# A two-network transformer stack in fp32 on one core: layer norm tile by tile, its affine part folded into the modulation columns

## The chip, the cores and the metric

The kernel is one program on one core of a Trainium2 chip. The metric is the device time of one execution in microseconds (us); the median over runs is compared. TensorE (PE) multiplies, VectorE (DVE) and ScalarE (ACT) do elementwise work, GpSimd (POOL) does a little of it and issues some transfers, SyncE (SP) only issues transfers.

## The reference

256 tokens of width 1024 pass through two networks, all in fp32.

```python
def _post_norm(x, y, gate, res_w, gain, bias):
    return _layer_norm(ALPHA * x + res_w * (1.0 + gate) * y, gain, bias)

for l in range(2):                                   # first network
    y = _swiglu(_modulate(x, sh1, sc1), ffn1...)     # 1024 -> 2816 -> 1024
    x = _post_norm(x, y, g1, 0.5, gain0, bias0)
    y = _token_mixer(_modulate(x, sh2, sc2), w_in, w_out)
    x = _post_norm(x, y, g2, 1.0, gain1, bias1)
    y = _swiglu(_modulate(x, sh3, sc3), ffn2...)
    x = _post_norm(x, y, g3, 0.5, gain2, bias2)
```

`_modulate(x, shift, scale)` is `x * (1 + scale) + shift`. Shift, scale and gate of each stage are rows of 1024 numbers: a condition vector times a 1024 x 1024 matrix, plus a bias. `_layer_norm` subtracts the mean of a token's 1024 numbers, multiplies with the inverse root of their variance, then multiplies with `gain` and adds `bias`. The second network has four more such stages: an attention and pooling mixer, a mixture of 16 experts that each take 32 of the 256 tokens (3 matrices of 1024 x 1024 per expert), a short convolution, and a second mixture of experts. Each ends in the same kind of post norm: ten in all.

## The kernel before

**Layout.** `x_tok` holds the residual, two token tiles (`t` = 0, 1) of 128 tokens by 1024. A stage needs it turned: PE transposes 128 x 128 blocks into PSUM banks 4 to 7, and ACT (banks 4, 5) and DVE (banks 6, 7) write them to `uT` with the modulation applied as a scale and a shift per partition (`turn`, L1020 on ACT, L1294 on DVE). For an FFN they write it twice, once in fp32 and once rounded to fp32r (`u_hi`), and DVE forms the difference `u_lo`; each product is then three fp32r products, high by high, low by high, high by low (L631, L643).

**Stages.** In order: FFN, mixer, FFN, FFN, mixer, FFN, attention mixer, experts, convolution, experts. The stage's result is summed in PSUM banks 0 to 3 (two per token tile). In the FFN loop, 22 hidden tiles run as gate/up (48 matmuls, L631) and down (12 matmuls, L643); ACT rounds the weights (`high_gate_up`, L1047), DVE takes the remainder (`low_gate_up`, L1347), and DVE also computes the modulation rows of later stages between them (L1263). `times_rows` (L668) is the output projection of a mixer: the chunk of the inner dimension is its outer loop, both token tiles are its inner one.

**Norm.** `norm(p, acc, ...)` on DVE waits for the whole sum, and then does each step for both token tiles before the next step: gate product (L1311), residual (L1315), statistics (L1319, L1322), variance plus epsilon (L1324), centre and gain (L1326), root on ACT (L1028), reciprocal (L1328), inverse root and bias (L1335). Then PE turns `x_tok` (L612), and ACT and DVE evacuate. ACT loads the bias row into `gate_row` when the gate product is done (L1026). `columns` (L1277) adds one to the scale.

**Queues.** SP issues the weights in program order with waits for free slots: `step_weights` for an FFN step (slots 0 to 2 and 3 to 5 in turn), `mod_chunk` for quarters of a modulation matrix (`W_mod`, two buffers), slots 6 to 11 for a mixer's 16 loads. A `mod_chunk` with `c == 0` first waits for `mod_taken`, that is, for DVE's sum of the row before (L1273), since it also loads `mod_bias`. In a mixer these quarters are multiplied on PE (`mod_quarter`, L589) between the projections (L688). POOL issues the shift and scale columns (L517), the gate and gain rows (L526, L527), and copies the condition for the next modulation job (`set_cond`, L532). The high and low weight parts (`parts`) lie over slots 8 to 11, `tmp` and `scr`. The two layers of the first network are a hardware loop on every engine.

## Time and profile before

| | |
|---|---|
| runs | 2713.0, 2719.28, 2723.32 us; median 2719.28 |
| profiled execution | 2719.25 us, its span 2717.6 |
| PE, DVE, ACT, POOL busy | 78%, 37%, 19%, 2% of the span |
| transfers | 758 MB, 279 GB/s over the span |

Busy time is a mean over stages with different limits; the windows below are cut at the stages' ends. PEclk is the TensorE clock that was granted, as a share of 2.4 GHz: 0.50 is its lower level, 1.2 GHz. In a timeline row the bracket gives the idle time before the instruction and what ended it; a row with a count merges instructions that follow each other.

### The profile page before, as it was taken

How to read it: one execution, taken by the hardware profiler on the slowest of the kernel's cores; microseconds unless marked ns; L12 is line 12 of the kernel's file. 1: busy time of each engine (PE TensorE's matmuls, PEld its weight loads, DVE VectorE, ACT ScalarE, POOL GpSimd, SP SyncE). 2: the span in 40 equal slices, each digit the busy share in tenths (PEclk: the TensorE clock that was granted, in tenths of full speed). 3: DMA queues.
4: the chain of work that ended last, by engine and by line, in shares of the span. 5: the costliest groups of instructions: out<-in, count | busy, mean ns of one | idle time of the engine just before them, and what ended most of it. 6: DMA issues, size and time to landing. Idle time of an engine off the chain costs nothing.

```text
span 2717.6 us, 34800 instructions
## 1 busy us (share of the span) xinstructions
PE 2130.7 (78%) x12924; PEld 1346.4 (50%) x12924; DVE 1009.7 (37%) x1599; ACT 506.8 (19%) x782; POOL 52.7 (2%) x83
## 2 busy tenths in 40 slices
PE   2899786799799798779977687777777967666665
PEld 1889345499699734469965332222225732111111
DVE  0777214578787702377734310000003131000002
ACT  0433012233333202133313110000000010000000
POOL 1000000000000000000010000000000000000000
PEclk8999897899899998889998787777778979888887
DMA  6787647178768663648862289999998339999997
GB/s 215 260 293 255 244 167 263 57 280 294 266 232 309 246 220 145 217 147 309 306 205 78 93 308 410 410 409 410 410 410 269 140 141 410 410 410 410 410 410 281
DMA packets 288864, 758.06 MB, mean 279 GB/s; under 512 B 17104, under 2 KB 124912, under 8 KB 288672
## 3 DMA queue, kind: packets, MB, share of 16 engines
q1 hardware_dynamic: 282368, 737.34, 72.0%
q0 software_dynamic: 5168, 16.05, 1.8%
q10 hardware_dynamic: 1264, 3.80, 0.4%
q8 instruction: 42, 0.69, 0.1%
q14 instruction: 22, 0.18, 0.0%
HBM read 755.94 MB, written 1.18 MB: 279 GB/s over the span
## 4 chain that ended last, share of the span: by engine, by line
PE 44%; DMA 24%; SPq 13%; DVE 9%; issue 4%; DVEq 4%; ACT 1%; ACTq 0%; POOL 0%; POOLq 0%
DMA W<-in_w_exp_up 16%; PE psum L631 13%; SPq L461 11%; PE psum L688 6%; PE psum L643 6%; DMA W_mod<-in_mod_w 5%; PE psum L668 4%; PE psum L987 3%; PE psum L589 2%; PE psum L926 2%; DVE parts L1347 2%; DMA W<-in_w_exp_down 1%; PE psum L828 1%; DVE mod_acc L1263 1%; SPq L465 1%
## 5 line engine op out<-in xcount | busy, mean ns | idle before, releaser
L631 PE MATMUL psum<-parts 128*128 128x256 f32 x4224 | 528.3, 285 | 43.3 <-DVE parts L1294 41.1
L631 PEld LDWEIGHTS psum<-parts 128*128 128x128 f32 x4224 | 524.0, 194 | 53.5 <-issue 42.1
L926 PE MATMUL psum<-W,scr 128*32 128x512 f32 x2048 | 305.8, 704 | 155.5 <-DMA W<-in_w_exp_up 151.3
L643 PE MATMUL psum<-parts 128*128 128x512 f32 x1056 | 257.7, 393 | 0.0
L926 PEld LDWEIGHTS psum<-W,scr 128*32 128x32 f32 x2048 | 52.3, 116 | 380.0 <-DMA W<-in_w_exp_up 304.2
L1347 DVE TENSOR_TENSOR parts<-W,parts 128x1024 fp32r<-128x1024 f32 x176 | 207.4, 1222 | 77.6 <-ACT parts L1047 77.6
L1682 DVE TENSOR_TENSOR scr<-scr,psum 128x256 f32<-128x256 f32 x32 | 13.5, 421 | 584.4 <-ACT scr L1212 584.4
L951 PE MATMUL psum<-W,scr 128*32 128x256 f32 x2048 | 177.1, 495 | 67.9 <-DMA W<-in_w_exp_down 52.7
L643 PEld LDWEIGHTS psum<-parts 128*128 128x128 f32 x1056 | 192.6, 188 | 45.2 <-issue 6.6
L1263 DVE SCALAR_TENSOR_TENSOR mod_acc<-W_mod,cond,mod_acc 128x1024 f32<-128x1024 f32 x140 | 179.9, 1285 | 56.9 <-DMA W_mod<-in_mod_w 36.7
L1047 ACT ACTIVATE parts<-W 128x1024 fp32r<-128x1024 f32 x176 | 175.8, 1051 | 107.5 <-issue 65.0
L688 PE MATMUL psum<-W,uT 128*128 128x512 f32 x384 | 177.5, 615 | 2.7 <-DVE uT L1294 2.7
L963 PE MATMUL psum<-scr 128*128 128x512 f32 x256 | 145.1, 719 | 31.7 <-DVE scr L1694 29.7
L951 PEld LDWEIGHTS psum<-W,scr 128*32 128x32 f32 x2048 | 71.8, 139 | 164.3 <-DMA W<-in_w_exp_down 86.4
L1212 ACT ACTIVATE scr<-psum 128x256 f32<-128x256 f32 x32 | 12.3, 383 | 599.4 <-PE psum L926 599.4
L1694 DVE COPY scr<-psum 32x256 f32<-32x256 f32 x64 | 27.3, 426 | 258.3 <-PE psum L951 257.9
L688 PEld LDWEIGHTS psum<-W,uT 128*128 128x128 f32 x384 | 73.2, 197 | 97.6 <-issue 95.1
L612 PE MATMUL psum<-k_ident,x_tok 128*128 128x128 f32 x160 | 36.2, 405 | 102.9 <-DVE x_tok L1335 101.6
L963 PEld LDWEIGHTS psum<-scr 128*128 128x128 f32 x256 | 57.0, 235 | 114.3 <-issue 61.7
L1356 DVE TENSOR_TENSOR parts<-W,parts 128x1024 fp32r<-128x1024 f32 x88 | 107.2, 1219 | 8.5 <-ACT parts L1056 8.5
L589 PE MATMUL psum<-W_mod,cond_now 128*32 128x256 f32 x768 | 61.6, 453 | 52.5 <-DMA W_mod<-in_mod_w 35.4
L1056 ACT ACTIVATE parts<-W 128x1024 fp32r<-128x1024 f32 x88 | 92.8, 1055 | 47.7 <-DVE mod_out L1273 18.5
(263 smaller groups left out, 1706.1 us busy)
## 6 DMA issues: line engine op xcount, KB each, us to landing
W_mod<-in_mod_w SPq DMA_DIRECT2D x128, 1024.0 KB, 6.5
W<-in_w_exp_down SPq DMA_DIRECT2D x128, 1024.0 KB
W<-in_w_exp_gate SPq DMA_DIRECT2D x256, 512.0 KB, 14.2
W<-in_w_exp_up SPq DMA_DIRECT2D x256, 512.0 KB, 15.7
W<-in_ffn_w_gate SPq DMA_DIRECT2D x44, 1024.0 KB, 9.5
W<-in_ffn_w_up SPq DMA_DIRECT2D x44, 1024.0 KB, 12.3
W<-in_ffn_w_down SPq DMA_DIRECT2D x44, 1024.0 KB, 10.1
W<-in_w_in SPq DMA_DIRECT2D x24, 1024.0 KB, 7.5
```

The source lines that it names most:

```text
L461: sp.dma_start(W[:, s, D * n:D * n + D], w[layer, ds(e, 1), P * s:P * s + P, :] .rearrange("a p n -> p (a n)")).then_inc(landed[s], 16)
L589: ins = pe.matmul(psum[32 * q:32 * q + 32, bank, 0:256], cond_now[:, 2 * c + kk, :], part(W_mod[:, c % 2, :], 0, 2, D)[:, kk, 256 * q:256 ...
L631: ins = pe.matmul(psum[:, 4 + t % 2, S * g:S * g + S], w[:, t % 2, g, kc, :], u[:, kc, :], start=(n == 0 and kc == 0), stop=(n == 2 and kc ...
L643: ins = pe.matmul(psum[:, 2 * tt + h, :], h_[:, t % 2, P * tt:P * tt + P], w[:, t % 2, 512 * h:512 * h + 512], start=(t == 0 and n == 0), ...
L668: ins = pe.matmul(psum[:, 2 * tt + h, :], src[:, kc, P * tt:P * tt + P], w[:, kk, 512 * h:512 * h + 512], start=(kc == 0), stop=(kc == KC ...
L688: ins = pe.matmul(psum[:, 4 + n % 4, :], uT[:, kc, P * t:P * t + P], part(W[:, s, :], 0, 4, 512)[:, kc % 4, :], start=(kc == 0), stop=(kc ...
L926: ins = pe.matmul(psum[32 * q:32 * q + 32, 4, :].rearrange("p (g n) -> p g n", g=2), xe_now[:, kc, :], w[:, :, q, :], start=(kc == 0), sto ...
L951: ins = pe.matmul(psum[32 * q:32 * q + 32, 6, 0:256], e_hT[:, c % 2, 32 * (c // 2):32 * (c // 2) + 32], part(W[:, s, :], 0, 2, D)[:, c % 2 ...
L963: ins = pe.matmul(psum[:, 2 * tt + h, :], GT[:, P * tt:P * tt + P], R[:, 512 * h:512 * h + 512], start=first, stop=True, skip_group_check= ...
L1047: ins = act.activation(gu_hi[:, t % 2, g, :, :], part(W[:, b + g, :], 0, KC, STEP)[:, :, P * (t % 2):P * (t % 2) + P], copy)
L1263: ins = dve.scalar_tensor_tensor(mod_acc[:, :], w, col, mod_acc[:, :], mul, add)
L1347: ins = dve.tensor_tensor(gu_lo[:, t % 2, g, :, :], part(W[:, b + g, :], 0, KC, STEP)[:, :, P * (t % 2):P * (t % 2) + P], gu_hi[:, t % 2, ...
```

## The change

- **Norm by token tile.** `norm` does gate product and moments of tile 0, then the gate product of tile 1, writes tile 0 of `x_tok`, then the moments of tile 1, and writes tile 1. The sum of tile 0 has a semaphore of its own (`acc_t0`), and `times_rows` finishes tile 0 before it begins tile 1.
- **No gain and no bias in it.** `x_tok` is written as (tmp - mean) * inverse root, by one `tensor_scalar`. `columns` builds `u_scale` = (1 + scale) * gain and `u_shift` = (1 + scale) * bias + shift from columns of 8 numbers per partition, and the evacuations use these. Only the last norm applies gain and bias itself.
- **`finish_x` on GpSimd** multiplies `x_tok` with the gain row and adds the bias row (four 128 x 1024 `tensor_tensor`, with a transfer of the bias row between them) once the stage has read the normalized `x_tok`; the next norm waits for it (`x_biased`).
- **Turning by tile.** PE turns tile 0 as soon as it is written; ACT alone evacuates its eight blocks (`turn_first`), and ACT and DVE share those of tile 1 (`turn_tiles`), which in an FFN are followed by one rounding of half of `uT` each.
- **Early weight parts.** A mixer's `w_out` goes to slots 0, 1, 2, 6, so that ACT and DVE form the high and low parts of the next FFN's first two tiles before the norm; in the same way between the two FFNs that follow each other (`then`). The second step of the FFN behind a mixer is loaded once the mixer's sum is done.
- **`mod_bias`** and the wait for `mod_taken` go from the first quarter of a modulation job to its last.
- The loop over the two layers is written out; PE turns the first tile of x between the context's products of the attention mixer.

The diff, cut to its core:

```diff
-MIX_S = (6, 7, 8, 9, 10, 11)
-MIX_SLOTS = len(MIX_S)
 MIX_IN_USES = IN_W * D // (P * 2048)
 MIX_USES = MIX_IN_USES + D * D // (P * 2048)
-PER_LAYER = [sum(1 for u in range(MIX_USES) if u % MIX_SLOTS == s) for s in range(MIX_SLOTS)]
+MIX_S = tuple(6 + u % 6 for u in range(MIX_IN_USES)) + (0, 1, 2, 6)
 SLOTS = 12
+UT_TURNS = [0, 1, 3, 4, 5, 7, 9, 10, 11, 12]
...
-                if c == 0:
+                if c == 3:
...
-                step_weights(l, k, 0, 0, base)
+                step_weights(l, k, 0, 0, max(base - 2, 1))
+                if k == 1:
+                    sp.wait_ge(m_pe.s, m_pe.at("out", l))
...
+            def finish_x(s, *read):
+                for r in read:
+                    pool.wait_ge(*r)
+                pool.wait_ge(gain_landed, s * 16)
+                for t in range(TT):
+                    ins = pool.tensor_tensor(x_tok[:, t, :], x_tok[:, t, :], gain_row[:, :], ALU.mult)
+                ins.then_inc(x_gained, 1)
+                pool.wait_ge(x_gained, s)
+                row(s, "ln_b", lnb_landed)
+                pool.wait_ge(lnb_landed, s * 16)
+                for t in range(TT):
+                    ins = pool.tensor_tensor(x_tok[:, t, :], x_tok[:, t, :], gain_row[:, :], ALU.add)
+                ins.then_inc(x_biased, 1)
...
+            columns(0, 0, 16 * 2)
+            for l in range(LAYERS):
+                mix_job = l * JOBS_LAYER + (FIRST_JOBS + PAIRS)
                 for k in range(3):
-                    turned = l * 4 + (1 + (k if k < 2 else 3))
-                    pool.wait_ge(tr_act, turned)
-                    pool.wait_ge(tr_dve, turned)
-                    columns(l * 9 + 3 * k, l * (9 * 16) + 16 * (3 * k + 2))
-                    rows(l * 3 + k, l * 9 + (3 * k + 2), l * (9 * 16) + 16 * (3 * k + 3))
+                    s = 3 * l + k
+                    if s:
+                        finish_x(s, (tr_pe, 16 * l + 4 * (0, 1, 3)[k] + 4))
+                        pool.wait_ge(x_biased, s)
+                    if s < 5:
+                        row(s + 1, "ln_g", gain_landed)
+                    gate(s, 9 * l + 3 * k + 2, 16 * (9 * l + 3 * k + 3))
+                    if k == 1:
+                        for j in range(1, PAIRS):
+                            set_cond(mix_job + j)
+                    if s < 5:
+                        columns(s + 1, 9 * l + 3 * k + 3, 16 * (9 * l + 3 * k + 5))
                     if k == 0:
-                        set_cond(l * JOBS_LAYER + (FIRST_JOBS + PAIRS))
-                    if k == 1:
-                        with pool.Fori(1, PAIRS) as j:
-                            set_cond(l * JOBS_LAYER + j + (FIRST_JOBS + PAIRS))
+                        set_cond(mix_job)
...
+            for s in range(6, 10):
+                at = MOD2 + 3 * (s - 6)
+                finish_x(s, *(((r_pe.s, r_pe.at("s7", (s - 7) // 2)),) if s in (7, 9) else ((tr_pe, 4 * (s + 3) + 4),)))
+                pool.wait_ge(x_biased, s)
+                row(s + 1, "ln_g", gain_landed)
+                gate(s, at + 2)
+                if s < 9:
+                    columns(s + 1, at + 3)
...
+            def turn_tile(ready, t):
+                pe.wait_ge(pn_x, ready)
+                for kc in range(KC):
+                    c = P * (kc % 4)
+                    ins = pe.transpose(psum[:, 4 + 2 * t + kc // 4, c:c + P], x_tok[:, t, P * kc:P * kc + P], ident[:, :])
+                    if kc % 4 == 3:
+                        ins.then_inc(tr_pe, 1)
...
+                at = []
+                for tt in range(TT):
+                    for kc in range(KC):
+                        if tt == 0 and kc % 2 == 0:
+                            at.append(slots(kc // 2))
+                        w = part(W[:, at[kc // 2], :], 0, 2, D)
+                        for h in range(2):
+                            ins = pe.matmul(psum[:, 2 * tt + h, :], src[:, kc, P * tt:P * tt + P],
+                                            w[:, kc % 2, 512 * h:512 * h + 512], start=(kc == 0), stop=(kc == KC - 1),
+                                            skip_group_check=True)
+                    if tt == 0:
+                        ins.then_inc(acc_t0, 1)
...
+                turn_tile(13 + t, t)
                 s = in_slot("in", MIXIN_S[2]) if t == 0 else MIXIN_S[2]
+                if t == 0:
+                    pe.wait_ge(pn_var, 11)
...
+            def turn_tiles(inst, s, split=False):
+                act.wait_ge(tr_pe, inst * 4 + 3)
+                for kc in range(KC // 2):
+                    src = psum[:, 6, P * kc:P * kc + P]
+                    ins = act.activation(uT[:, kc, P:S], src, copy, bias=u_shift[:, kc:kc + 1], scale=u_scale[:, kc:kc + 1])
+                if split:
+                    act.drain()
+                    ins = act.activation(u_hi[:, 0:4, :], uT[:, 0:4, :], copy)
+                ins.then_inc(tr_act, 1)
+            def turn_first(inst, s):
+                act.wait_ge(cols_ready, s + 1)
+                for kc in range(KC):
+                    if kc % 4 == 0:
+                        act.wait_ge(tr_pe, inst * 4 + kc // 4 + 1)
+                    src = psum[:, 4 + kc // 4, P * (kc % 4):P * (kc % 4) + P]
+                    ins = act.activation(uT[:, kc, 0:P], src, copy, bias=u_shift[:, kc:kc + 1], scale=u_scale[:, kc:kc + 1])
+                ins.then_inc(tr_first, 1)
+            def root(s, t):
+                act.wait_ge(pn_var, 2 * s + t + 1)
+                act.activation(rstd[:, t:t + 1], inv[:, t:t + 1], ACT.Sqrt).then_inc(pn_sqrt, 1)
+            def norm_turn(s, inst, split=False):
+                root(s - 1, 0)
+                turn_first(inst, s)
+                root(s - 1, 1)
+                turn_tiles(inst, s, split)
...
+                if then is not None:
+                    high_gate_up(*then, 0)
                 silu(TILES - 1)
+                if then is not None:
+                    high_gate_up(*then, 1)
...
+            def columns(s, evacuated=None):
+                dve.wait_ge(cols_landed, s * 64 + 32)
+                if evacuated is not None:
+                    dve.wait_ge(*evacuated)
+                if s:
+                    dve.scalar_tensor_tensor(u_scale[:, :], scale_c[:, :], 1.0, gain_c[:, :], add, mul)
+                    dve.scalar_tensor_tensor(u_shift[:, :], scale_c[:, :], 1.0, bias_c[:, :], add, mul)
+                    dve.drain()
+                    dve.tensor_tensor(u_shift[:, :], u_shift[:, :], shift_c[:, :], add).then_inc(cols_ready, 1)
...
+            def turn_tiles(inst, split=False):
+                dve.wait_ge(tr_pe, inst * 4 + 4)
+                for kc in range(KC // 2, KC):
+                    src = psum[:, 7, P * (kc % 4):P * (kc % 4) + P]
+                    ins = dve.tensor_scalar(uT[:, kc, P:S], src, u_scale[:, kc:kc + 1], u_shift[:, kc:kc + 1], mul, add)
+                if split:
+                    dve.wait_ge(tr_first, 1 + UT_TURNS.index(inst))
+                    dve.drain()
+                    ins = dve.tensor_copy(u_hi[:, 4:8, :], uT[:, 4:8, :])
...
+            def norm(s, summed, alpha, res, eps, last=False):
+                dve.wait_ge(rows_landed, s * 16 + 16)
                 if res is not None:
                     dve.tensor_scalar(gate_row[:, :], gate_row[:, :], 1.0, res, add, mul)
                     dve.drain()
...
+                if last:
+                    dve.wait_ge(gain_landed, 160)
+                    dve.wait_ge(lnb_late, 16)
+                def gated(t):
+                    dve.wait_ge(*summed[t])
+                    dve.tensor_tensor(part(tmp[:, t, :], 0, 2, 512), psum[:, 2 * t:2 * t + 2, :], part(gate_row[:, :], 0, 2, 512), mul)
+                def moments(t):
+                    dve.drain()
                     dve.scalar_tensor_tensor(tmp[:, t, :], x_tok[:, t, :], alpha, tmp[:, t, :], mul, add)
...
+                    dve.drain()
                     for h in range(2):
                         dve.bn_stats(stats[:, 2 * t + h, :], tmp[:, t, 512 * h:512 * h + 512])
...
+                    dve.drain()
                     dve.bn_aggr(mv[:, t, :], stats[:, 2 * t:2 * t + 2, :])
...
+                    dve.drain()
+                    dve.tensor_scalar(inv[:, t:t + 1], mv[:, t, 1:2], eps, None, add).then_inc(pn_var, 1)
+                def scaled(t):
+                    dve.wait_ge(pn_sqrt, 2 * s + t + 1)
+                    dve.reciprocal(inv[:, t:t + 1], rstd[:, t:t + 1])
+                    if last:
+                        dve.scalar_tensor_tensor(tmp[:, t, :], tmp[:, t, :], mv[:, t, 0:1], gain_row[:, :], sub, mul)
+                        dve.drain()
+                        dve.scalar_tensor_tensor(x_tok[:, t, :], tmp[:, t, :], inv[:, t:t + 1], bias_late[:, :], mul, add
+                                                 ).then_inc(pn_x, 1)
+                    else:
+                        dve.drain()
+                        dve.tensor_scalar(x_tok[:, t, :], tmp[:, t, :], mv[:, t, 0:1], inv[:, t:t + 1], sub, mul).then_inc(pn_x, 1)
+                gated(0)
+                if s:
+                    dve.wait_ge(x_biased, s)
+                moments(0)
+                gated(1)
+                scaled(0)
+                moments(1)
+                scaled(1)
...
+            for l in range(LAYERS):
+                s = 3 * l
+                turn_tiles(4 * l, split=True)
                 ffn(l, 0)
-                norm(l * 3, (pe_down, l * (2 * TILES) + (1 + TILES)), ALPHA, 0.5, LN_EPS)
-                turn(l * 4 + 1, l * 3 + 1)
+                columns(s + 1, (tr_act, 4 * l + 2))
+                norm(s, ((acc_t0, s + 1), (pe_down, l * (2 * TILES) + (1 + TILES))), ALPHA, 0.5, LN_EPS)
+                turn_tiles(4 * l + 1)
                 mixer(l)
-                norm(l * 3 + 1, (m_pe.s, m_pe.at("out", l)), ALPHA, 1.0, LN_EPS)
-                ffn(l, 1)
-                norm(l * 3 + 2, (pe_down, l * (2 * TILES) + (1 + 2 * TILES)), ALPHA, 0.5, LN_EPS)
-            dve.engine_nop().then_inc(tr_dve, 1)
-            turn(9, 6)
+                for t in range(2):
+                    low_gate_up(l, 1, t)
+                columns(s + 2, (tr_act, 4 * l + 3))
+                norm(s + 1, ((acc_t0, s + 2), (m_pe.s, m_pe.at("out", l))), ALPHA, 1.0, LN_EPS)
+                turn_tiles(4 * l + 3, split=True)
+                ffn(l, 1, (1, 0) if l == 0 else None)
```

## Rows read from the trace of the kernel before

**Rows 1.** The page's chain that ended last, by engine.
```profile
PE 44%; DMA 24%; SPq 13%; DVE 9%; issue 4%; DVEq 4%; ACT 1%; ACTq 0%; POOL 0%; POOLq 0%
```

**Rows 2.** Windows by stage: length, busy time by engine, PEclk, DMA share, rate.
```profile
273.00:290.50 17.50, 3.91 (x16) 3.24 (x16) 14.21 (x21) 3.42 (x6) 1.10 (x2) 0.61 0.98 361
...
501.70:523.50 21.80, 3.74 (x16) 3.20 (x16) 21.03 (x30) 8.06 (x14) 1.10 (x2) 0.63 0.34 111
523.50:716.60 193.10, 193.08 (x1360) 179.07 (x1360) 147.96 (x176) 70.60 (x85) 1.79 (x2) 0.99 0.74 262
716.60:740.00 23.40, 3.78 (x18) 3.23 (x17) 21.25 (x30) 10.78 (x16) 1.10 (x2) 0.63 0.81 288
...
1375.40:1401.30 25.90, 12.30 (x66) 10.35 (x63) 14.57 (x21) 8.19 (x17) 2.01 (x3) 0.80 1.04 383
...
1531.20:1548.90 17.70, 3.94 (x16) 3.26 (x17) 14.55 (x21) 4.70 (x7) 1.61 (x3) 0.60 0.86 324
...
1575.00:2052.00 477.00, 360.97 (x2272) 113.68 (x2264) 40.53 (x113) 28.16 (x69) 1.78 (x2) 0.75 1.02 404
```

**Rows 3.** Timeline, all engines, from the first FFN's end to the mixer.
```profile
266.98 5.63 PE L643 MATMUL psum<-parts 128*128 128x512 f32 x24
...
268.81 0.68 DVE L1307 TENSOR_SCALAR gate_row<-gate_row 128x1024 f32<-128x1024 f32 x1
272.65 2.36 DVE L1311 TENSOR_TENSOR tmp<-psum,gate_row 128x1024 f32<-128x1024 f32 x2 [3.16 <-PE psum L643]
...
275.11 2.36 DVE L1315 SCALAR_TENSOR_TENSOR tmp<-x_tok,tmp 128x1024 f32<-128x1024 f32 x2
...
277.54 2.47 DVE L1319 BATCH_NORM_STATS2 stats<-tmp 128x6 f32<-128x512 f32 x4
...
283.24 2.48 DVE L1335 SCALAR_TENSOR_TENSOR x_tok<-tmp,rstd,gate_row 128x1024 f32<-128x1024 f32 x2 [0.16 <-issue]
...
285.77 3.43 PE L612 MATMUL psum<-k_ident,x_tok 128*128 128x128 f32 x15 [0.72 <-DVE x_tok L1335]
...
286.71 1.93 ACT L1020 ACTIVATE uT<-psum,shift_c,scale_c 128x256 f32<-128x256 f32 x4 [5.86 <-PE psum L612]
...
288.42 1.90 DVE L1294 TENSOR_SCALAR uT<-psum,scale_c,shift_c 128x256 f32<-128x256 f32 x4 [2.62 <-PE psum L612]
...
290.58 9.70 PE L688 MATMUL psum<-W,uT 128*128 128x512 f32 x22 [1.37 <-DVE uT L1294]
```

**Rows 4.** Instructions of two lines, ns min/median/max.
```profile
L1206 ACT ACTIVATE scr<-psum,shift_c,scale_c x8: 457/457/457, 1567.8 to 2228.0; 128x128 f32<-128x128 f32 x8
...
L1669 DVE TENSOR_SCALAR scr<-psum,scale_c,shift_c x8: 409/410/411, 1568.6 to 2228.4; 128x128 f32<-128x128 f32 x8
```

**Rows 5.** Chain in order of time behind the first mixer.
```profile
523.52 13.73 PE psum L631 x96
...
539.99 5.03 PE psum L631 x42
```

**Rows 6.** Timeline of the attention mixer's start: the context's products.
```profile
1388.63 8.58 PE L816 MATMUL psum<-W,scr 128*128 128x256 f32 x32 [11.48 <-ACT scr L1155]
```

**Rows 7.** PE's waits from 290 to 470, and the timeline there.
```profile
PE psum L589 <- DMA W_mod<-in_mod_w: 9.3, 3, 3.3
...
317.66 0.61 PE L589 MATMUL psum<-W_mod,cond_now 128*32 128x256 f32 x8
...
324.53 1.09 SPq L379 DMA_DIRECT2D W_mod<-in_mod_w  x2
...
329.80 1.79 PE L589 MATMUL psum<-W_mod,cond_now 128*32 128x256 f32 x16 [3.26 <-DMA W_mod<-in_mod_w]
```

**Rows 8.** Timeline of GpSimd's copies, and of DVE at the second.
```profile
16.47 0.40 POOL L532 COPY cond_now<-cond 128x256 f32<-128x256 f32 x1 [7.46 <-DVEq L1556]
...
257.24 1.22 POOL L532 COPY cond_now<-cond 128x256 f32 x1 [135.81 <-DVE mod_acc L1263]
...
256.99 2.56 DVE L1347 TENSOR_TENSOR parts<-W,parts 128x1024 fp32r<-128x1024 f32 x2
```

354 lines of the change are left out of this document (167 added, 187 removed).

## The prediction

> **What bounds the kernel now.** I read the chain that ended last first: PE has 44% of it, transfers and SP's queue 37%, DVE 9% [rows 1]. Then the windows by stage [rows 2]. An FFN is PE alone: 193.08 us busy of 193.10, clock 0.99. The expert stages are the transfers: 477 us at 404 GB/s, DMA share 1.02. Neither is touched by the change in its body. Between stages neither works: in the window of 17.5 us behind an FFN PE is busy 3.9 at a clock of 0.61, and DVE is busy 14.2; behind a mixer the window is 21.8, between the two FFNs that follow each other 23.4, at the attention mixer's start 25.9, and 17.7 before the experts (two more like it, 17.6 to 17.8, at both ends of the convolution). Nothing runs beside such a gap that could absorb it: the next stage starts later by all of it, in an expert stage too, since its slots are full before it starts and the stream goes on only when the first expert frees them. So the change is worth what it takes from nine such gaps, less what it adds at the last norm and inside the stages.
>
> The timeline of one gap [rows 3] gives the prices, in us per token tile: gate product 1.2 (2.36 for two), residual 1.2, statistics 1.25, aggregate to variance 0.5 (from 280.0 to where DVE goes on at 280.5, read off the same stretch), centring and final product 1.25 each. From the sum's end T = 272.6 to the first projection at 290.6 it is 18.0.
>
> **A new gap, step by step.** Let G be the start of tile 0's gate product. Its variance is out at G + 4.3 (1.2 + 1.2 + 1.25 + 0.5 and drains of 0.1). Tile 1's gate product follows, at T at the earliest, 1.2. Root, reciprocal and drain take 0.3. The normalization is one `tensor_scalar`; the only 128 x 1024 one from SBUF to SBUF took 0.68 with constants as its scalars [rows 3], a pass at DVE's plain rate 1.2; here the scalars are columns. I take 0.75. So tile 0 is written at X = max(G + 4.3, T) + 2.2. Then three things run at once: DVE makes tile 1's moments (3.1); PE turns eight blocks at 0.23 each (3.43 for 15), 1.85; ACT, from the fourth block on, evacuates eight of 128 x 128. One of these took 0.457 and one of DVE's 0.409 [rows 4]; four of double width took 1.93 and 1.90, 0.48 apart [rows 3]. Between them I take 0.35 apart (bound: 0.46), 2.9 for eight, so ACT is done at X + 4.15, roots tile 1, and tile 1 is written at X + 5.6. ACT, not DVE, sets that. Turning 1.85 and four evacuations 1.4 follow: the stage starts at X + 9.2, an FFN at X + 10.1 with DVE's rounding of half of `uT` (0.7). By place:
>
> - FFN to mixer, twice. Tile 0 of the last down product is complete 6 matmuls of 0.235 before T [rows 3], G = T - 1.4, X = T + 5.1, start T + 14.4: 3.6 saved each, 7.2.
> - Mixer to FFN, twice. With the token tile outside, tile 0's sum is ready half of the projection (14 us) before T, its moments are hidden behind it, X = T + 2.3, start T + 12.4. The two weight tiles that DVE splits in the gap now (four operations of some 1.2) are split during the projection, when DVE is idle. Before 21.8: 9.4 each, 18.8.
> - FFN to FFN. The split of the next weight tiles lies around the last `hidden`; DVE is free at T + 0.9, X = T + 7.4, start T + 17.6. Before 23.4: 5.8.
> - FFN to attention mixer. Turning tile 0 waits for the context's evacuation (T + 5.8 with the root put between), the first context product (half of 8.6 [rows 6]) covers the moments of tile 1, ACT's eight evacuations end at T + 9.9, tile 1 is written at T + 11.3, turned by T + 12.8, the second context product ends at T + 17.1. Before 25.9: 8.8.
> - Attention mixer and convolution to experts: X = T + 2.3, start T + 11.5, before 17.7: 6.1 each, 12.2.
> - Experts to convolution: both sums end together, G = T, X = T + 6.5, start T + 15.8, before 17.8: 2.0.
> - The last norm keeps gain and bias. Tile 1 is written at T + 14.9 (4.3 + 1.2 + 0.3 + 2.6 + 3.1 + 0.4 + 0.3 + 2.7) where it now is at 13.1: 1.8 lost.
> - The kernel's first turn: one rounding pass takes the place of four double writes; I give it 1 (0 to 2).
>
> **The modulation quarters.** In a mixer PE waits 9.3 us for `W_mod`, three times [rows 7]. Quarter c = 2 is done at 318.3, yet SP issues the next job's first quarter only at 324.5, behind DVE's row sum; PE then stands 3.26 at 329.8. With that wait at the last quarter SP issues at 318.4; a landing of 5.3 makes 323.7, PE comes at 326.5. Two of the three waits go (3.26 and 3.15), the third, a buffer that PE itself has just freed, stays: 6.4 per mixer, 12.8.
>
> **What it adds on GpSimd.** `finish_x` is four two-input operations of 1024. No row has one; the nearest is a copy of 256: 0.40 alone, 1.22 beside DVE's subtraction of two SBUF operands, which itself went on at its usual pace, 2.56 for two [rows 8]. So one costs from 1.6 (four copies) to 9.8 (four copies beside DVE, two inputs); I take 2.4. With the bias row's landing `finish_x` is some 18 us, hidden in the shortest stage (convolution, 118). In an FFN it starts when tile 1 is turned, exactly when DVE rounds `uT` and forms `u_lo`. If the two exclude each other, DVE waits between 0.2 and two operations, 4.8; I take 1.7 for three FFNs, 5 in all. Later in the FFN DVE has 45 us of slack [rows 2]. In the other stages DVE reads PSUM or idles then.
>
> The row shows GpSimd as the loser. The Trainium skill (SBUF — State Buffer, Who interferes with whom) says that the port pair is an exclusive lock: a DVE instruction with two SBUF inputs, or in a two-port mode, and a GpSimd one that reads SBUF block each other whole, whoever starts first. The row agrees that one blocks; by that rule GpSimd, which starts first here, would win, and the cost would be near the upper bound, 14 instead of 5. The skill (GPSIMD Engine Reference, Elementwise — side-by-side cycle accounting) gives 4497 ns for a `tensor_tensor` of 2048, which would be some 2.2 us here, an estimate no run here shows.
>
> **Behind SP's new wait** (the sum of the mixer, before the second FFN step): gate and up of that step are issued at T and ACT wants them when the first gate/up is done, T + 12.4 + 6.9. A landing after 12 leaves 7 us; no cost. `set_cond` and the gate row stand behind `finish_x` on POOL, see below.
>
> **Sum.** 7.2 + 18.8 + 5.8 + 8.8 + 12.2 + 2.0 - 1.8 + 1 + 12.8 - 5 = 61.8. The profiled execution took 2719.25 (span 2717.6, 1.65 around it), as good as the median, so 2657.5.
>
> **Rivals.**
> - *The vector steps are dearer* (20%). The normalization at the plain rate costs 0.5 twice in each of nine gaps, 9; evacuations 0.46 apart 1.2 each, 11; GpSimd in front of DVE 9 more. About two of the three: 2677; all: 2687.
> - *The clock stays up* (14%). Now each gap has PE idle for 12 us and then turns at 0.23 per block; behind a mixer the first 96 gate/up matmuls take 13.7 where 0.12 apiece makes 11.5 [rows 5]. With PE's pauses cut to 2 to 5 us the clock may stay at 2.4 GHz where the gap is short: about 1.3 in the turns and 2.2 at an FFN's start, 16 in all: 2641. Against it: that FFN starts at the low clock now although PE turned x only a few us before. The Trainium skill (TensorE: Matmul & The Clock Gate, Why this matters for your kernels) advises to keep pauses short for this; the trace agrees that the long ones end at the low clock.
> - *No change* (3%): another in-order wait eats it, for example ACT held by `high_gate_up` for late weights ahead of the last `silu`, or norms that wait for `x_biased`; some 2715.
> - *Slower* (3%): `set_cond` for a mixer's second quarter job stands behind `finish_x`. From tile 1 turned, T + 13, to that quarter at T + 50 are 36 us; less the row's landing (7) and issues there are 7 us per operation. Beyond that each us per operation stalls PE by 4 in two mixers; from 15 us per operation on, the kernel is slower, at 18 it takes 2745. DVE does almost nothing there, so 1.6 is nearer than 9.8, and 15 lies above both.
>
> **Numbers.** The forecast has 60%, 2657 with its own range 2645 to 2670. For 8 in 10 I take in the dearer vector steps and the higher clock: 2637 to 2684. No change is within 0.5% (13.6 us), about what a measurement here can tell: faster 0.94, same 0.03, slower 0.03.
>
> **What would show it.** Windows from a sum's end to the next stage: 14.4, 12.4, 17.6, 17.1, 11.5, 15.8, and 14.9 at the end. `tensor_scalar` into `x_tok` near 0.75. The wait of the root of tile 1 behind eight ACT evacuations. PE's waits for `W_mod` down to 3 per mixer. GpSimd's operations near 2.4 and DVE's rounding and `u_lo` late by up to two of them. FFN windows still 193 and expert windows still 477. The forecast is wrong if GpSimd holds DVE through the FFN's loop, if the written-out layers make the engines wait for instructions, or if PE starts a stage later than X + 9.2 although all of these are as priced.

## The result, and the profile of the changed kernel

The changed kernel takes 2647.59 us (median, 2645.96 to 2649.14), the kernel before 2717.13 (2713.0 to 2723.32) on the same chip: a ratio of 0.9742, 95% interval 0.9721 to 0.9764. Forecast was 2657, a gain of 61.8 us; about 70 were measured. The profiled executions differ by as much, 2717.6 and 2647.4 us of span, so the 70.2 can be laid out stretch by stretch.

The chain that ended last, by engine, for the changed kernel; [rows 1] had 44% for PE and 4% for DVE's queue:

```profile
PE 54%; DMA 20%; SPq 12%; DVE 6%; issue 3%; ACT 3%; DVEq 1%; POOL 0%; ACTq 0%; POOLq 0%
```

The same kernel's windows by stage, columns as in [rows 2]: FFN to mixer, mixer to FFN, an FFN, FFN to FFN, attention mixer to experts, and both expert stages from their first weight product on.

```profile
262.00:276.30 14.30, 3.95 (x17) 3.16 (x17) 10.10 (x19) 4.70 (x14) 1.57 (x1) 0.61 0.95 343
477.80:490.70 12.90, 3.96 (x17) 3.17 (x17) 9.03 (x16) 7.00 (x16) 3.19 (x2) 0.59 0.92 319
490.70:685.90 195.20, 193.36 (x1360) 178.33 (x1360) 159.30 (x183) 74.40 (x89) 13.05 (x10) 0.99 0.86 299
685.90:703.60 17.70, 3.95 (x17) 3.15 (x17) 13.46 (x23) 7.15 (x17) 3.13 (x2) 0.57 0.37 119
...
1468.10:1478.80 10.70, 3.08 (x17) 2.47 (x17) 7.32 (x14) 5.35 (x14) 0.00 (x0) 0.75 0.91 356
1503.90:1981.60 477.70, 366.38 (x2272) 100.81 (x2272) 40.95 (x116) 28.23 (x69) 14.66 (x11) 0.75 1.02 404
2152.00:2629.80 477.80, 343.52 (x2272) 97.01 (x2272) 40.52 (x113) 28.23 (x69) 11.67 (x8) 0.80 1.00 400
```

Every gap is shorter, the FFN is not: 195.2 against 193.1, and PE is no longer busy for all of it. The clock in the gaps is as low as it was (0.57 to 0.61; 0.63 ahead of the second experts), except ahead of the first experts (0.75) and at the attention mixer's start, where it is 0.80 as before.

The table is worked out from the traces: a gap runs from the end of a stage's last matmul to the start of the next stage's first one. "Bias row alone" is the kernel before with one edit and "last version" the changed kernel with three, both from the experiments below.

| stretch, us | before | bias row alone | changed | saved | forecast | last version |
|---|---|---|---|---|---|---|
| kernel's start to first FFN | 76.3 | 70.3 | 68.6 | 7.7 | 1 | 68.8 |
| FFN 1 | 196.3 | 192.7 | 193.5 | 2.8 | 0 | 193.7 |
| gap to mixer | 18.0 | 18.0 | 14.3 | 3.7 | 3.6 | 13.4 |
| mixer 1 | 211.1 | 196.9 | 201.5 | 9.6 | 6.4 | 199.2 |
| gap to FFN | 21.8 | 21.8 | 12.9 | 9.0 | 9.4 | 12.0 |
| FFN 2 | 193.1 | 193.0 | 195.2 | -2.1 | -1.7 | 195.3 |
| gap FFN to FFN | 23.3 | 22.7 | 17.7 | 5.6 | 5.8 | 16.8 |
| FFN 3 | 193.6 | 192.7 | 193.9 | -0.2 | -1.7 | 193.5 |
| gap to mixer | 18.0 | 18.0 | 14.3 | 3.7 | 3.6 | 13.4 |
| mixer 2 | 209.0 | 200.8 | 200.7 | 8.3 | 6.4 | 198.2 |
| gap to FFN | 21.8 | 21.8 | 12.6 | 9.2 | 9.4 | 12.0 |
| FFN 4, gap, attention mixer | 348.8 | 350.8 | 343.0 | 5.8 | 7.1 | 342.5 |
| gap to experts | 17.8 | 18.1 | 10.7 | 7.1 | 6.1 | 10.3 |
| experts 1, routing included | 503.1 | 499.9 | 502.8 | 0.3 | 0 | 499.2 |
| gap to convolution | 17.8 | 17.8 | 16.0 | 1.8 | 2.0 | 15.2 |
| convolution | 117.9 | 118.1 | 118.2 | -0.2 | 0 | 117.1 |
| gap to experts | 17.8 | 17.8 | 10.8 | 7.0 | 6.1 | 10.3 |
| experts 2, routing included | 495.7 | 494.9 | 503.1 | -7.5 | 0 | 498.9 |
| last norm and output | 16.3 | 16.3 | 17.6 | -1.3 | -1.8 | 17.6 |

The eight gaps that stand alone give 47.1 us where 46.0 were forecast, and the ninth, to the attention mixer, is 16.9 for 17.1. The rest of the agreement is luck: start, FFN 1 and the two mixers give 28.4 where 13.8 were expected, and the second expert stage loses 7.5 that no step had.

DVE's timeline behind the first mixer in the changed kernel:

```profile
477.86 1.23 DVE L1422 TENSOR_TENSOR tmp<-psum,gate_row 128x1024 f32<-128x1024 f32 x1 [9.33 <-PE psum L726]
479.00 0.15 DVE L1437 RECIPROCAL inv<-rstd 128x1 f32<-128x1 f32 x1
479.24 0.81 DVE L1445 TENSOR_SCALAR x_tok<-tmp,mv,inv 128x1024 f32<-128x1024 f32 x1
480.14 1.23 DVE L1426 SCALAR_TENSOR_TENSOR tmp<-x_tok,tmp 128x1024 f32<-128x1024 f32 x1
481.44 1.29 DVE L1429 BATCH_NORM_STATS2 stats<-tmp 128x6 f32<-128x512 f32 x2
...
483.08 0.15 DVE L1433 TENSOR_SCALAR inv<-mv 128x1 f32<-128x1 f32 x1
484.34 0.17 DVE L1437 RECIPROCAL inv<-rstd 128x1 f32<-128x1 f32 x1 [1.11 <-ACT rstd L1102]
484.59 0.81 DVE L1445 TENSOR_SCALAR x_tok<-tmp,mv,inv 128x1024 f32<-128x1024 f32 x1
...
488.90 1.51 DVE L1399 CAST parts<-uT 128x1024 fp32r<-128x1024 f32 x1
490.50 4.35 DVE L1407 TENSOR_TENSOR parts<-uT,parts 128x1024 fp32r<-128x1024 f32 x2
```

Tile 0 is written 2.2 us after the sum's end at 477.8, as forecast (2.3). The normalization takes 0.81, not 0.75. The bracket on the second reciprocal is the wait forecast for tile 1: its variance is there at 483.2, its root comes at 484.1, behind ACT's eight evacuations (2.90 us). The last two rows take about twice what they need (0.69 and 2.36, see below), beside GpSimd's two multiplications, which run from 487.5 to 492.6.

### The profile page after: what moved, and what is told of

It is laid out like the page before. It is cut to its first block, busy times and chain, and to the rows that moved or that the text cites. A ratio compares the mean times of both kernels' runs of the same rounds, so it can differ in the third digit from the quotient of the medians.

```text
span 2647.4 us, 34365 instructions
## 1 busy us (share of the span) xinstructions
PE 2153.5 (81%) x12924; PEld 1331.9 (50%) x12924; DVE 999.8 (38%) x1608; ACT 526.3 (20%) x858; POOL 161.5 (6%) x144
## 4 chain that ended last, share of the span: by engine, by line
PE 54%; DMA 20%; SPq 12%; DVE 6%; issue 3%; ACT 3%; DVEq 1%; POOL 0%; ACTq 0%; POOLq 0%
PE psum L686 18%; DMA W<-in_w_exp_up 17%; SPq L471 12%; PE psum L698 8%; PE psum L749 7%; PE psum L726 4%; PE psum L1050 3%; PE psum L989 2%; PE psum L628 2%; DMA W_mod<-in_mod_w 1%; DMA W<-in_w_exp_down 1%; PE psum L891 1%; PE psum L659 1%; ACT uT L1096 1%; PE psum L1001 1%
## 5 line engine op out<-in xcount | busy, mean ns | idle before, releaser
L686 PE MATMUL psum<-parts 128*128 128x256 f32 x4224 | 528.8, 285 | 34.5 <-ACT parts L1086 21.8
L989 PE MATMUL psum<-W,scr 128*32 128x512 f32 x2048 | 353.2, 790 | 154.0 <-DMA W<-in_w_exp_up 149.1
L1463 DVE TENSOR_TENSOR parts<-W,parts 128x1024 fp32r<-128x1024 f32 x176 | 215.4, 1267 | 69.6 <-ACT parts L1126 69.4
L1026 PE MATMUL psum<-scr 128*128 128x512 f32 x256 | 118.4, 605 | 31.7 <-DVE scr L1828 29.6
L553 POOL TENSOR_TENSOR x_tok<-x_tok,gain_row 128x1024 f32<-128x1024 f32 x18 | 43.3, 2424 | 1190.2 <-PE psum L659 870.9
L1476 DVE TENSOR_TENSOR parts<-W,parts 128x1024 fp32r<-128x1024 f32 x88 | 107.2, 1218 | 10.3 <-ACT parts L1138 10.3
L1145 ACT ACTIVATE att<-psum 128x256 f32<-128x256 f32 x88 | 33.8, 384 | 381.2 <-PE psum L686 381.2
L1026 PEld LDWEIGHTS psum<-scr 128*128 128x128 f32 x256 | 46.0, 189 | 93.0 <-issue 45.9
## 6 DMA issues: line engine op xcount, KB each, us to landing
W<-in_w_exp_gate SPq DMA_DIRECT2D x256, 512.0 KB, 14.7
```

The source lines that it names most:

```text
L686: ins = pe.matmul(psum[:, 4 + t % 2, S * g:S * g + S], w[:, t % 2, g, kc, :], u[:, kc, :], start=(n == 0 and kc == 0), stop=(n == 2 and kc ...
L989: ins = pe.matmul(psum[32 * q:32 * q + 32, 4, :].rearrange("p (g n) -> p g n", g=2), xe_now[:, kc, :], w[:, :, q, :], start=(kc == 0), sto ...
L1026: ins = pe.matmul(psum[:, 2 * tt + h, :], GT[:, P * tt:P * tt + P], R[:, 512 * h:512 * h + 512], start=first, stop=True, skip_group_check= ...
L1463: ins = dve.tensor_tensor(gu_lo[:, t % 2, g, :, :], part(W[:, b + g, :], 0, KC, STEP)[:, :, P * (t % 2):P * (t % 2) + P], gu_hi[:, t % 2, ...
L1476: dve.tensor_tensor(d_lo[:, t % 2, :], part(W[:, b + 2, :], 0, 2, D)[:, t % 2, :], d_hi[:, t % 2, :].bitcast(F32), sub).then_inc(lo_d, 1)
```

## Experiments

Each comes with its ratio to the kernel before, timed on its own chip; the changed kernel stands at 0.9742. One thousandth is 2.7 us, and a ratio's interval is two of them wide to each side, so the stretches of the traces say where a difference lies, and the ratio whether the sum bears it out.

### The bias row first again, everywhere

```diff
-                if c == 3:
+                if c == 0:
                     if first != 0:
                         sp.wait_ge(mod_taken, job)
```

> The changed kernel with one edit undone: the bias row of a modulation job is again asked for before the job's first quarter, behind the wait for the job before it. Theory A, the prediction's sum: only the two mixers lose, 6.4 us each, and the kernel's start 1 us, in all about 14, so about 2661 us. Theory B, from the trace of the changed kernel: the start also hangs on this wait (the first FFN starts at 68.6 us in place of 76.3), so the start gives back 6 to 7 us and the two mixers 14 (their waits were 9.3 and 9.8 us, and are 3.3 and 1.9), in all about 20, so about 2668 us, and the first FFN's matmuls start at about 75 us.

Measured: 2678.47 us, ratio 0.985 (0.9827 to 0.9874), 29 us over the changed kernel by the ratios, 30.3 by the traces. Both theories were too low. PE's waits in the first mixer, us in total, times, longest, first in the changed kernel, then here:

```profile
PE psum L628 <- DMA W_mod<-in_mod_w: 3.3, 1, 3.3
```

```profile
PE psum L628 <- DMA W_mod<-in_mod_w: 10.5, 5, 3.0
```

The mixers lose 10.2 and 7.6 us, the start 3.1, FFN 1 5.1 and the other FFNs 2.0, 0.4 and 2.7. In FFN 1 the link goes over DVE, which sums the modulation's quarters there. Its waits and PE's in that stage, in this kernel:

```profile
DVE mod_acc L1355 <- DMA W_mod<-in_mod_w: 13.4, 8, 3.6
```

```profile
PE psum L686 <- DVE parts L1463: 3.4, 4, 1.2
```

and the two lines that answer to them in the kernel before:

```profile
DVE mod_acc L1263 <- DMA W_mod<-in_mod_w: 11.4, 8, 4.0
```

```profile
PE psum L631 <- DVE parts L1347: 1.8, 3, 1.2
```

The changed kernel has neither in FFN 1, nor has the kernel before with the bias row's edit alone. DVE works in order: it stands for a quarter, and the parts of the next weights, behind that sum, are late for PE. These waits of PE explain 3.4 of the 5.1 us; the other 1.7 lie in PE's own busy time (195.1 against 193.4), and what makes that longer is not shown.

### The bias row first in the first jobs alone

```diff
-                if c == 3:
+                if c == (3 if first is None else 0):
```

> The changed kernel with the bias row ahead of the first quarter, behind its wait, only for the modulation jobs at the kernel's start; the mixers keep the late one. Theory A: about 1 us slower, so no difference that can be measured (2648 to 2649). Theory B: 6 to 7 us slower, about 2654 us, and the first FFN's matmuls start at about 75 us in place of 68.6. Rival to both: the 7.7 us at the start come from weight parts and columns made ahead of the first transposes, which this run leaves in place; then it stays at 68.6 us.

Measured: 2651.44 us, ratio 0.9754 (0.9731 to 0.9777). The sums can't be told apart (3 us by the ratios, 1.3 by the traces), but the stretch can: the first FFN starts at 72.5 in place of 68.6, between the two theories. So 3.9 of the start's 7.7 us hang on this in the changed kernel, or about 5, since in the later runs that leave this order alone the start takes 67.0 to 67.6. SP's queue at the start, in the kernel before and in the changed one, shows it:

```profile
30.00 0.55 SPq L376 DMA_DIRECT2D mod_bias<-in_mod_b  x1
30.59 9.94 SPq L379 DMA_DIRECT2D W_mod<-in_mod_w  x4
55.45 0.40 SPq L396 DMA_DIRECT2D W<-in_ffn_w_gate  x1
```

```profile
20.28 12.05 SPq L387 DMA_DIRECT2D W_mod<-in_mod_w  x4
34.45 0.55 SPq L384 DMA_DIRECT2D mod_bias<-in_mod_b  x1
35.03 0.44 SPq L387 DMA_DIRECT2D W_mod<-in_mod_w  x1
48.96 0.37 SPq L404 DMA_DIRECT2D W<-in_ffn_w_gate  x1
```

The second job's quarters used to be asked for from 30.6 on, when the first job's row was taken; now the next four are asked for from 20.3 on, and the first weights of the FFN leave 6.5 us earlier.

### The bias row's edit alone, on the kernel before

```diff
                 if first is None or 2 * first + c // 2 > 0:
                     sp.wait_ge(mod_freed[c % 2], 2 * job + c // 2)
-                if c == 0:
+                if c == 3:
```

> The kernel before with one edit alone, the bias row of a modulation job asked for ahead of its last quarter and no longer ahead of its first. Theory A, the prediction's: the two mixers give 6.4 us each and the start 1, 14 us, 2703 us. Theory B: what the undoing in the changed kernel cost comes back whole, about 31 us (start 3, first FFN 5, mixers 10 and 8, later FFNs 4), 2686 us. Theory C: it depends on when the weights' fills fall due; in the kernel before, whose FFN stages were no longer than the changed kernel's, only the start's 3 and the mixers' 18 come, 2696 us.

Measured: 2682.19 us, ratio 0.9856 (0.984 to 0.9871), 39 us by the ratio (35 to 43), 35.2 by the traces. The table's third column says where: start 6.0, FFN 1 3.6, mixers 14.2 and 8.1. Theory B came nearest. One line moved, by itself, is worth half of the change or more. What the norms, the fold and GpSimd add on top of it is 31 us (0.9742 over 0.9856), where the forecast had 48 for them. The two parts don't simply add up: without the moved line the rest of the change gives 41 us (ratio 0.985, in the run with the bias row first again), 39.8 by the traces, and the line moved last adds 29.

### The bias row behind the last quarter

```diff
+                src = A["mod_w"][ds(job, 1), 256 * c:256 * c + 256, :]
+                sp.dma_start(part(W_mod[:, c % 2, :], 0, 2, D), ...
                 if c == 3:
                     if first != 0:
                         sp.wait_ge(mod_taken, job)
```

> The changed kernel with the bias row asked for behind the job's last quarter in place of ahead of it, so that no quarter waits for the job before to be taken. Theory A: the 3.3 and 1.9 us that TensorE still waits for a quarter in the mixers come from this wait, and both go, 5 us, 2642 us. Theory B: they are the time that the transfers themselves take, and nothing changes, 2647 us.

Measured: 2642.63 us, ratio 0.9722 (0.9701 to 0.9743). The first mixer's wait for a quarter is 1.5 us here in place of 3.3, but in the other runs that have the changed kernel's order it is 1.9 to 3.5. The mixers took 198.8 and 198.2 us; in those runs they scatter from 200.4 to 204.3 and from 197.1 to 202.7. So the wait did not go, and neither theory is shown: a gain of 2 us is as well borne out as one of 5, and so is nearly none.

### One more pass over each tile

```diff
                     else:
+                        dve.scalar_tensor_tensor(x_tok[:, t, :], tmp[:, t, :], mv[:, t, 0:1], gate_row[:, :], sub, mul)
                         dve.drain()
                         dve.tensor_scalar(x_tok[:, t, :], tmp[:, t, :], mv[:, t, 0:1], inv[:, t:t + 1], sub, mul).then_inc(pn_x, 1)
```

> The changed kernel with one pass more over each tile between the reciprocal and the last operation of the norm (128x1024, the form that the fold took away; its result is written over), for nine of the ten norms. Theory A: both tiles' passes lie on the path, 1.27 us each, 2.5 us in each gap, in eight gaps 20 us (the gap into the second expert stage counts nothing, since the stream of weights ends when it ends), about 2668 us. Theory B: only the first tile's pass counts (the second hides behind ScalarE's eight evacuations), 1.3 us in each gap, about 10 us, 2658 us.

Measured: 2665.46 us, ratio 0.9809 (0.9787 to 0.9831), 18 us over the changed kernel. DVE's timeline behind the first mixer, in this kernel:

```profile
479.16 1.27 DVE L1444 SCALAR_TENSOR_TENSOR x_tok<-tmp,mv,gate_row 128x1024 f32<-128x1024 f32 x1
480.50 0.81 DVE L1446 TENSOR_SCALAR x_tok<-tmp,mv,inv 128x1024 f32<-128x1024 f32 x1
...
485.61 0.16 DVE L1437 RECIPROCAL inv<-rstd 128x1 f32<-128x1 f32 x1 [1.10 <-ACT rstd L1102]
485.69 1.26 DVE L1444 SCALAR_TENSOR_TENSOR x_tok<-tmp,mv,gate_row 128x1024 f32<-128x1024 f32 x1
```

The gaps grow by 2.4, 2.3, 2.4, 2.4, 2.6, 2.3, 2.0 and 3.1 us: theory A. Both passes lie on the path, since tile 1's wait for its root stays at 1.10 and everything before it moves. So the pass that the fold takes out of the path is worth about 2.4 us in a gap. The gap ahead of the second expert stage counted like the others; the expectation that the stream would swallow it was wrong, as the stage behind it was no shorter (505.6 against 503.1).

### Tile 0 waits for both sums

```diff
+                summed = (summed[1], summed[1])
                 dve.wait_ge(rows_landed, s * 16 + 16)
```

> The changed kernel in which the norm's first tile also waits for the sum of both tiles (the order of the matmuls stays). Theory A: where the rows' product runs tile by tile (two mixers, the second mixer, the conv), gate, residual and moments of tile 0 (1.23, 1.23, 1.37, 0.2, 0.15 and the drains, 4.4 us) move behind the end of the product, in the other five gaps 1.3 us of them do. Three times 4.4 and five times 1.3 are 20 us, the conv's 4.4 vanish in the stream of the second expert stage: about 2667 us. Theory B: if the stream doesn't hide it, 2672 us. Theory C: root and evacuation waits absorb most of it, under 10 us.

Measured: 2666.99 us, ratio 0.9819 (0.9799 to 0.9838), 21 us over the changed kernel. The gaps behind the four tile-by-tile products grow by 4.3, 4.9, 4.8 and 4.7 us; those from FFN to mixer by 1.4; from FFN to FFN by nothing, where DVE is still at the last `hidden`, and from experts to convolution by nothing, where both sums end together. So what the early sum of tile 0 hides is as it was priced (4.3 from gate to variance), and again the gap ahead of the second expert stage counts whole. The total is theory A's, but by luck: A left that gap out and counted two gaps that did not grow.

### Tile 1's root in the midst of the evacuations

```diff
+                    if kc == 5 and then_root:
+                        root(s - 1, 1)
                     src = psum[:, 4 + kc // 4, P * (kc % 4):P * (kc % 4) + P]
...
-                root(s - 1, 1)
```

> The changed kernel with tile 1's square root issued after five of ScalarE's eight evacuations of tile 0, in place of after all eight. Theory A: tile 1's reciprocal waits for ScalarE in every gap (0.65 to 1.11 us of idle VectorE), the root then starts as soon as the variance is there, and each gap is 0.4 to 0.8 us shorter, over eight gaps 4 to 5 us, 2643 us. Theory B: the three evacuations that now come behind the root are late for tile 1's or for TensorE, and nothing is gained: 2647 us.

Measured: 2638.41 us, ratio 0.9717 (0.9701 to 0.9734), 7 us under the changed kernel. Timeline behind the first mixer, in this kernel:

```profile
480.17 0.15 DVE L1433 TENSOR_SCALAR inv<-mv 128x1 f32<-128x1 f32 x1
480.36 0.20 ACT L1104 ACTIVATE rstd<-inv 128x1 f32<-128x1 f32 x1
...
480.46 1.14 ACT L1098 ACTIVATE uT<-psum,u_shift,u_scale 128x128 f32<-128x128 f32 x3
480.59 0.16 DVE L1437 RECIPROCAL inv<-rstd 128x1 f32<-128x1 f32 x1 [0.27 <-ACT rstd L1104]
```

The 1.11 us of idle DVE are 0.27, and the gaps are 0.4 to 0.9 us shorter, 5.9 in eight: theory A. The three evacuations behind the root hold nobody up.

### GpSimd's work on the residual cut to 8 columns

```diff
-                    ins = pool.tensor_tensor(x_tok[:, t, :], x_tok[:, t, :], gain_row[:, :], ALU.mult)
+                    ins = pool.tensor_tensor(x_tok[:, t, 0:8], x_tok[:, t, 0:8], gain_row[:, 0:8], ALU.mult)
```

and the same for the addition of the bias.

> The changed kernel with GpSimd's four passes over the residual cut to 8 of 1024 columns (so gain and bias are left out of most of the residual; its four row fetches and all waits stay). It prices GpSimd's 129 us of work. Theory A, the prediction's: it costs 1.7 us at the start of each of three FFN stages and nothing worth naming elsewhere, so about 5 us faster, 2642 us. Theory B, from the run in which the same work only began later and nothing was gained: the contention on VectorE is paid also in the middle of the FFN stages, and their lengths (195.8, 192.6 and 192.8 us from the start of one to its end) fall by 1 to 2 us each beside the 1.5 at their starts, in all 8 to 10 us, 2638 us. In the expert stages nothing changes, since the stream of weights sets them.

Measured: 2639.82 us, ratio 0.9728 (0.9709 to 0.9748); by the ratios the gain over the changed kernel is 4 us and could be nothing, by the traces it is 12.7, but these are this run's fastest execution and the changed kernel's slowest. So the sum does not decide between the theories; the stretches say more. DVE's timeline at the start of the second FFN, in this kernel:

```profile
485.95 0.69 DVE L1399 CAST parts<-uT 128x1024 fp32r<-128x1024 f32 x1
486.73 2.36 DVE L1407 TENSOR_TENSOR parts<-uT,parts 128x1024 fp32r<-128x1024 f32 x2
```

Against 1.51 and 4.35 in the changed kernel. The gaps ahead of FFN 2, 3 and 4 are 1.3, 0.8 and 1.1 us shorter, FFN 2 and 3 by 2.0 and 1.5, the stretch from FFN 4 on by 3.2, and PE is busy without a pause again (this kernel's window of FFN 2, columns as above):

```profile
486.90:680.10 193.20, 193.20 (x1360) 179.26 (x1360) 153.07 (x183) 75.21 (x90) 4.99 (x8) 0.99 0.87 305
```

In the expert stages nothing changes (502.5 and 502.8).

What FFN 2 had lost is in PE's waits of the changed kernel there, and the rows of DVE and of GpSimd say why:

```profile
PE psum L686 <- DVE parts L1463: 1.1, 2, 0.8
PE psum L686 <- DVE parts L1407: 0.7, 1, 0.7
```

```profile
501.46 3.37 DVE L1463 TENSOR_TENSOR parts<-W,parts 128x1024 fp32r<-128x1024 f32 x1 [0.72 <-ACT parts L1126]
```

```profile
501.35 5.75 POOL L559 TENSOR_TENSOR x_tok<-x_tok,gain_row 128x1024 f32<-128x1024 f32 x2 [7.81 <-DMA gain_row<-in_ln_b]
```

The two additions began 10.6 us into the stage, just ahead of DVE's two subtractions for the next weights, which took 3.4 us each in place of 1.2. In FFN 3 of the same kernel the additions came 6.3 us into the stage and met neither of them, and PE waited only the 0.5 us at the start; in the run with one more pass they came 8.6 us into FFN 2, the waits at L1463 were gone, and FFN 2 took 193.5. So 1.8 of FFN 2's 2.0 us are waits that hang on where the additions fall, and of FFN 3's 1.5 only 0.5 are.

### The same work later in the FFN

```diff
-                        finish_x(s, (tr_pe, 16 * l + 4 * (0, 1, 3)[k] + 4))
+                        finish_x(s, (tr_pe, 16 * l + 4 * (0, 1, 3)[k] + 4), *(((u_low, 2 * l + k // 2 + 1),) if k != 1 else ()))
```

> The changed kernel with one wait more: in the three FFN stages in which GpSimd applies gain and bias to the residual, it starts only when VectorE has made the low parts of the input. Theory A: GpSimd slows VectorE there (the cast takes 1.51 us in place of 0.69, the two subtractions 4.35 in place of 2.36) and TensorE waits for them, so the start of each of the three gives back 1.5 us, in all 4.5, about 2643 us, with the cast at 0.7 and the subtractions at 2.4 us again. Theory B: the same contention is paid later in the stage, where VectorE makes the parts of the next weights while TensorE is busy; then the gain is smaller or nothing, 2646 to 2648 us.

Measured: 2649.83 us, ratio 0.9749 (0.9725 to 0.9774): no gain. The three gaps are 1.1, 0.8 and 1.1 us shorter, and FFN 2, FFN 3 and the stretch from FFN 4 are 1.6, 1.6 and 2.8 longer: theory B, though FFN 3 took as long in two runs without this edit (195.4 and 195.7). Timelines of DVE and of GpSimd in FFN 2, in this kernel:

```profile
500.60 5.30 POOL L559 TENSOR_TENSOR x_tok<-x_tok,gain_row 128x1024 f32<-128x1024 f32 x2 [4.45 <-DMA gain_row<-in_ln_b]
```

```profile
501.48 0.42 DVE L1485 TENSOR_TENSOR att<-att,psum 128x256 f32<-128x256 f32 x1 [0.26 <-ACT att L1145]
501.97 1.67 DVE L1487 CAST parts<-att 128x256 fp32r<-128x256 f32 x1
503.71 2.47 DVE L1489 TENSOR_TENSOR parts<-att,parts 128x256 fp32r<-128x256 f32 x1
```

The two additions cover 500.6 to 505.9; they took 2.89 and 2.45 us. DVE's operation with an operand in PSUM took 0.42 beside them, as ever. The cast needs 0.29 and ended at 503.6, just behind the end of the first addition; the subtraction of two SBUF operands needs 0.42 and ended at 506.2, just behind the second. Both stand ahead of the modulation's sum on DVE, which so frees its buffer later, and a later quarter is late. Timelines of DVE and of PE, 15 us on:

```profile
519.19 1.28 DVE L1355 SCALAR_TENSOR_TENSOR mod_acc<-W_mod,cond,mod_acc 128x1024 f32<-128x1024 f32 x1 [3.29 <-DMA W_mod<-in_mod_w]
```

```profile
524.25 0.98 PE L686 MATMUL psum<-parts 128*128 128x256 f32 x6 [3.35 <-DVE parts L1463]
```

The 3.7 us that DVE loses beside GpSimd come back as 3.29 of waiting for a transfer and 3.35 of PE. That the lost DVE time is what made this transfer late was not tried by itself; the run that cuts GpSimd's work has neither wait. So what was gained ahead of the stages was lost in them. The Trainium skill (SBUF — State Buffer, Who interferes with whom) says that such instructions of DVE and GpSimd shut each other out for their whole length; this trace agrees, with DVE held to the end of GpSimd's operation both times. It shows the other order too: GpSimd's first multiplication, begun 0.2 us behind a subtraction of DVE at 489.4, took 3.24 us and DVE's the usual 1.22.

### Rows out of the expert stages

```diff
...
+                if early:
+                    gate(s, MOD2 + 3 * (s - 6) + 2)
+                    pool.dma_start(bias_early, A["ln_b"][s - 1:s, :].to_broadcast([P, D])).then_inc(lnb_landed, 16)
+                if s == 9:
+                    pool.dma_start(bias_late, A["ln_b"][9:10, :].to_broadcast([P, D])).then_inc(lnb_late, 16)
                 for r in read:
                     pool.wait_ge(*r)
...
```

> The changed kernel with five of the rows that GpSimd fetches in the two expert stages taken out of the stretch in which the weights' stream is the bound: gate row and bias row are asked for before the wait for the gather (the bias row goes into a free half of the modulation buffer), the very last bias row too, and the first stage's next gain row only behind it. Theory A: the expert stages are set by TensorE and its waits on weights alone, rows of 0.5 MB beside a stream of 180 MB change nothing, 2647 to 2648 us. Theory B: both stages run at the rate of the stream (404 GB/s), each row of 0.52 MB costs 1.3 us there, so three rows less in each stage give 3.9 us each, in all about 8 us, 2640 us; the stretch from the first expert's first matmul to the last expert's end falls from 477.9 to about 474 us in both. The 471.4 us of the kernel before in the second stage, which had none of the rows in it, is the bound from below: 13 us.

Measured: 2638.24 us, ratio 0.971 (0.9686 to 0.9735), 9 us under the changed kernel. The queues in the second expert stage from its first weight product on: before (471.3 us), changed (477.8), here (473.4):

```profile
DMA packets 50884, 188.82 MB, mean 401 GB/s; under 512 B 4800, under 2 KB 4800, under 8 KB 50880
...
q1 hardware_dynamic: 50880, 188.76, 100.5%
```

```profile
DMA packets 51460, 190.92 MB, mean 400 GB/s; under 512 B 4864, under 2 KB 4864, under 8 KB 51456
...
q1 hardware_dynamic: 50880, 188.76, 99.2%
q0 software_dynamic: 576, 2.10, 1.1%
```

```profile
DMA packets 51028, 189.34 MB, mean 400 GB/s; under 512 B 4816, under 2 KB 4816, under 8 KB 51024
...
q1 hardware_dynamic: 50880, 188.76, 100.1%
q0 software_dynamic: 144, 0.52, 0.3%
```

The weights are the same 188.76 MB at the same rate. The kernel before fetched its rows for this stage at 2201 us, in the idle end of the convolution's gap; the changed one must first read the residual in the gather, so all four rows (2.10 MB) go into the stream. At 400 GB/s that is 5.2 us of the 6.5; with one row left (0.52 MB, 1.3 us) the stage is 2.1 longer than before. Experts 2 gained 4.8 us here, experts 1 only 1.8, where theory B had 3.9 for each. Rows were not as dear in the first expert stage: three of them (1.57 MB) lie in its stream in the changed kernel, and from its first weight product on it grew only from 477.3 to 477.8 us. That stream also fetches the convolution's weights ahead, and 1.3 MB less of them fell into the stage.

### Two and three of the edits together

> The changed kernel with two of the edits tried before together: GpSimd's rows outside the weights' stream in the two expert stages, and tile 1's root after five evacuations. Theory A: the two add up (rows 7 to 9 us, roots 7 us), about 2632 us, with the gaps at 14.7, 25.7 and 16.3 us and the expert stages at 501 and 498 us. Theory B: the parts that lie ahead of the two expert stages are swallowed by the stream, since each stage ends with it, and the roots keep only the gaps ahead of the mixers and FFNs, about 2635 us.

Rows and root together: 2633.65 us, ratio 0.968 (0.9665 to 0.9694), 17 us under the changed kernel, where the two alone add up to 16. The total lies between the theories (2632 and 2635). The gaps are 13.4, 12.0 and 16.8 (the expectation's 14.7, 25.7 and 16.3 were none of these), the two ahead of the experts 10.3 in place of 10.7 and 10.8, and the stages behind them, at 499.6 and 499.2 against 501.0 and 498.3 with the rows alone, are not longer by more than the scatter: that speaks for theory A and does not settle it.

> The changed kernel with the three edits that gave something: rows outside the weights' stream, tile 1's root after five evacuations, and the bias row behind the last quarter. Theory A: the bias row's 5 us come on top of 2634 us, about 2629 us, with the mixers at about 198 us each. Theory B: the time given back at the quarters in the mixers was only the scatter of one stage from run to run (197 to 203 us in the runs so far), and the three together measure as the two did, 2632 to 2636 us.

With the bias row behind the last quarter as well: 2631.03 us, ratio 0.9673 (0.966 to 0.9686), the fastest version, 19 us under the changed kernel. It can't be told from the version with two edits: theory B holds, or a gain of 2 us. The table's last column is this run.

## Why the prediction came out as it did

**The gaps: right, by their mechanism.** All nine are within 1 us of their forecast. The run that makes tile 0 wait shows the hidden 4.3 us, the run with one more pass the 1.2 per tile, and the run with the root in the midst the wait behind ACT's eight evacuations, of which 0.4 to 0.9 us could be had. Evacuations 0.35 us apart were right (eight in 2.90), the normalization was 0.06 short. The last norm lost 1.3 for 1.8. 

**The modulation quarters: the mis-sized term.** The step read the 9.3 us of PE's waits in a mixer and kept one of three: 12.8 for both mixers, and nothing anywhere else (the 1 us at the start was for the first turn, not for this). The edit alone measured 35 us by its trace: 22.3 in the mixers, 6.0 at the start, 3.6 in FFN 1, 3.2 in the first expert stage, which has no such wait and whose length scatters by 3 us and more between runs. Two things were not read. The wait in SP's queue stands also in the kernel's start, where PE, DVE and the first weights all stand behind it; and in the FFNs, where PE's rows had shown 193.1 us without a pause because I looked at the second FFN [rows 2]. FFN 1 took 196.3, DVE stood there eight times for a quarter, 11.4 us, and PE for DVE's parts 1.8. In the mixers the waits themselves fell about as forecast, from 9.3 and 9.8 us to 3.3 and 1.9 in the changed kernel, and to 1.7 and 3.1 with the edit alone. But the first mixer got shorter by more than that (9.6 us, 14.2 with the edit alone): PE's busy time fell too, from 179.3 to 176.2, and to 172.8 in the run with the edit alone. What of that is the edit and what the scatter of the clock from run to run (0.89 to 0.92 in this stage) stays open.

**GpSimd: right in size at the place looked at, wrong beyond it.** An operation takes 2.35 us alone (2.4 taken), and DVE's cast and subtractions at an FFN's start are late by 0.8 and 2.0, PE by 1.5 in FFN 2 (0.8 ahead of its first product, 0.7 behind it; 1.7 taken). But "later in the FFN DVE has 45 us of slack" was false comfort: slack of an in-order engine on average does not help the one operation that PE waits for next, and in FFN 2 the additions met it. With the work cut, the three gaps, FFN 2, FFN 3 and the stretch from FFN 4 on are 9.9 us shorter together, between the 5 of the sum and the 14 that the prediction worked out for GpSimd in front; some of that is scatter. Moving the work later only moved the loss. In the table part of this is hidden: the moved bias row gave FFN 2, 3 and 4 back 2.0, 0.4 and 2.7 us at the same time, by the run that undoes it.

**The second expert stage: the step that was missing.** The text said that nothing but the gaps moves in the expert stages, and that `finish_x` with its bias row is hidden. Its operations are; its DMAs are not, since the stage is bound by the transfers and GpSimd's queue carries four rows of 0.5 MB that stand behind the wait for the gather. It costs 7.5 us in the second stage (6.5 from its first weight product on), and 4.8 came back when three of the rows were asked for earlier. In the first stage the same kind of rows cost next to nothing, so the words held there.

**The rivals.** Dearer vector steps and no change did not occur. "The clock stays up" came true in one gap of the profiled execution: ahead of the first experts the eight turns of tile 0 took 1.09 us in place of 1.97. In three other runs they took 1.97 there, and the gap 11.15 us in place of 10.7, so the higher clock is worth 0.45 in this gap, where the rival had 1.3. At the FFNs it did not come true: the clock is 0.57 to 0.60 in the gaps ahead of FFN 2, 3 and 4. The slower rival needed 15 us per GpSimd operation; the longest took 3.4.

**What stays open.** Not settled are the 3.1 and 2.5 us by which the expert stages were longer in the run with one more pass, how much the last bias row edit is worth, and whether PE's busy time in the mixers and in FFN 1 changes with the place of the bias row or only scatters.

## What to carry to other kernels

A wait in the queue that issues transfers is paid by everyone behind it: list every place where the queue passes it, loops and the start as well, and don't price it by the consumer's waits in one stage. When work is moved into another stage, price its DMAs by what bounds that stage; half a megabyte cost 1.3 us beside the saturated stream of the second expert stage. And for an off-path engine that holds up a feeder of TensorE, the moment decides, not the feeder's idle share: the same two additions cost FFN 2 about 1.1 us where they met the subtractions for the next weights, and nothing that shows as a wait where they came 2 to 4 us earlier.

## What the runs showed of the hardware

- GpSimd's `tensor_tensor` of 128x1024 floats in SBUF: 2.33 to 2.37 us alone, up to 3.4 beside DVE. A DVE cast or a subtraction of SBUF operands that met one already running ended behind its end, by no more than its own usual length (0.29 us became 1.67, 0.42 became 2.47, 1.22 became 3.4); one with an operand in PSUM is not held (0.42).
- DVE's `tensor_scalar` over 128x1024 with two columns as scalars took 0.81 us, with constants 0.68 [rows 3].
- The eight turns of tile 0 took 1.97 us behind the first mixer, 1.75 behind the second, 1.09 ahead of the first experts and 1.62 ahead of the second, each time after 2.28 us of idle TensorE and a long run of work. Behind the first mixer they took from 1.09 to 1.97 in the other runs with that same gap, and ahead of the first experts 1.09 or 1.97. So the granted level at one place of the program differs from execution to execution. Tile 1's took 1.97 in all four, after 3.4 to 3.8 us more of idleness.
- Rows of 0.52 MB fetched beside the weight stream of the expert stages of the changed kernel took 7.3 to 7.5 us from issue to landing when asked for alone, and 7.9 to 12.4 in groups of two and three.
